# First layer's up groups 4 to 7 in pairs, by seven block products in place of eight

## The chip, the cores and the metric

The kernel runs on one core of a Trainium2 chip. The metric is the device time of one execution in microseconds; before the change it is 982.56 us, the median of 3 runs (982.32 to 982.68). All arithmetic is float32.

## The reference

Two layers of a first block (a mixer with two branches, then an MLP) are followed by a second block. Sequence length is 256, width 1024, inner width 4096. What matters here is the first block's MLP, once for each of two layers; `rms` stands for the normalisation:

```
u = relu(rms(x) * g_mlp @ w_up) ** 2      # [256, 1024] @ [1024, 4096]
x = x + u @ w_down                        # [256, 4096] @ [4096, 1024]
```

The scale of a row is left out of the products and put on the result, since the square makes it a factor of the row.

## The kernel before

**Three products for one.** A float32 product is made of three matmuls on a shorter format. Each operand is split into an upper part (a rounded copy) and a lower part (the remainder): upper times upper, upper times lower, lower times upper. Of weights, a *piece* is 128 partitions x 4 blocks x 512 columns (1 MB). ScalarE copies it into `w_hi` (`split` at L1737), VectorE subtracts that from the loaded piece into `w_lo` (`split` at L2160). Both rings hold three pieces (`SPLIT_RING`), so the split of piece p waits until TensorE has used piece p − 3.

**TensorE.** The 256 rows are two tiles of 128. One piece with one tile of rows is 4 blocks x 3 = 12 matmuls of 128x128 by 128x512, called a *block product* here; the first 8 of a piece need only `w_hi`, the last 4 `w_lo` (`products_upper`, L964 to L983). Each group f of `w_up` (512 columns) has two pieces, so four block products and 48 matmuls (`mlp_up`). `mlp_down` adds the same number into four banks that stay open. `MLP_STEPS` sets the order: up 0, 1, 2, down 0, up 3, down 1, up 4 and so on.

**Rows of a group.** ScalarE takes the relu from PSUM (L1895), VectorE multiplies it by the bank (L2388) into `u_rows`, SyncE stores the rows to `u_bounce` and fetches them back by blocks of 32 (`store_up`, `fetch_up`), VectorE transposes the blocks (L2336, `up_rows_turn`), ScalarE makes the upper part (L1903) and VectorE the remainder (L2404). Then `mlp_down` can use them.

**Order.** Each engine's order is written out by hand, and each works in that order. ScalarE and VectorE call `step(p)` in a loop over `MLP_STEPS`, which splits piece p + 2; `TURNED_IN` says between which splits a group's rows are transposed. SyncE issues all transfers; a load waits until the piece that lay in its place (a ring of four) has been split by VectorE. GpSimd does nothing in this stage but two short powers.

The first layer's MLP begins at about 201 us; its first up group ends at 212.5, and its last matmul starts at 375.5.

Of the kernel before, what the change touches and what calls it, by code (L numbers as in the profile page):

```python
# [6 lines left out]
F32 = mybir.dt.float32  # L7
# [74 lines left out]
UP_PIECE = [PIECE_MLP + 2 * MLP_STEPS.index(("up", f)) for f in range(F_GROUPS)]  # L82
DOWN_PIECE = [PIECE_MLP + 2 * MLP_STEPS.index(("down", f)) for f in range(F_GROUPS)]
# [3 lines left out]
PIECES = PIECE_MLP + 4 * F_GROUPS  # L87
ANGLES_AT = 2
TURNED_IN = {2: 0, 3: 1, 14: F_GROUPS - 1}
TURNED_IN.update({MLP_STEPS.index(("up", f)) + (3 if f < F_GROUPS - 2 else 2): f for f in range(2, F_GROUPS - 1)})  # L90

# [6 lines left out]
E_PIECE = DEPTH * PIECES  # L98
# [22 lines left out]
RAW_SLOTS = [p % RAW_RING for p in range(RAW_SWITCH)] + list(RAW_ODD)  # L121
# [63 lines left out]
def build_program(nc, ins, consts, where, out):  # L185
    ctx = ExitStack()
    with ctx:
# [86 lines left out]

        def raw_at(p):

            slot = RAW_SLOTS[p]
            if slot < RAW_KEPT:
# [74 lines left out]
        u_bounce = [nc.dram_tensor(f"u_bounce{i}", [T * P, COLS], F32, kind="Internal").ap() for i in range(2)]  # L353
# [151 lines left out]
        up_half = sem("up_half")  # L505
        up_hi = sem("up_hi")
# [89 lines left out]
        def last_piece(n):  # L596

            l, u = divmod(n, USES)
            if l < DEPTH:
                if u < W_IN_GROUPS:  # L600
                    return l * PIECES + 2 * u + 1
                if u in USE_YB:
                    return l * PIECES + PIECE_B[USE_YB.index(u)] + 1
                if u in USE_YA:
                    return l * PIECES + PIECE_A[USE_YA.index(u)]
                if u < USE_UP:
                    return l * PIECES + PIECE_O + 2 * (u - USE_O) + 1
                return l * PIECES + UP_PIECE[u - USE_UP] + 1
# [85 lines left out]
        def _(sp):  # L694
# [7 lines left out]
            def load(piece):  # L702
# [18 lines left out]
                elif p == 2:  # L721
                    sp.dma_start(raw_at(2)[:, 0:KP // 2, :], piece[:, 0:KP // 2, :]).then_inc(third_landed, 16)
# [6 lines left out]
                n[0] += 1  # L729

# [68 lines left out]
            def store_up(l, g):  # L799
# [3 lines left out]
                else:  # L803
                    for t in range(T):
                        sp.wait_ge(out_free[t], l * USES + USE_UP + g + 1)
                store_rows(u_bounce[g % 2].rearrange("(t p) n -> p t n", p=P), u_rows, rows_stored)

            def fetch_up(l, g):

                sp.wait_ge(rows_stored, 16 * (STORES * l + 2 * T + g + 2))  # L810
                sp.wait_ge(blocks_turned, MOVES * l + 2 + g + 1)
                fetch_blocks(u_moved, u_bounce[g % 2], row_blocks)

            def row_blocks_piece(w, c, half):

                return w.rearrange("(p k) n -> p k n", p=P)[:, half * KP:half * KP + KP, c * COLS:(c + 1) * COLS]

            for l in range(DEPTH):
# [14 lines left out]
                for i, (kind, f) in enumerate(MLP_STEPS):  # L833
                    if l == DEPTH - 1 and i == 9:
                        for t in range(T):
                            sp.wait_ge(out_free[t], l * USES + USE_UP)
                        sp.dma_start(g_final, ins["g_final"].partition_broadcast(P)).then_inc(g_first_landed, 16)
                        sp.dma_start(g_pre[0], ins["pre_norm_g_2"][0].partition_broadcast(P)).then_inc(g_first_landed, 16)
                        for b, w in enumerate(("o_c_re_2", "o_c_im_2")):
                            sp.dma_start(c_in[:, b, :, :], ins[w][0].rearrange("(s g) p o -> (g p) s o", g=2)).then_inc(s5_landed, 16)  # L840
                        for b, w in enumerate(("o_b_re_2", "o_b_im_2")):
                            sp.dma_start(b_in[:, b, :, :], ins[w][0].rearrange("(j g) i p -> (g i) j p", g=8)).then_inc(s5_landed, 16)
                    for c in range(2):
                        if kind == "down":
                            load(square_piece(ins["w_down"][l, f * COLS:(f + 1) * COLS, :], c, 0))
                        else:
                            load(square_piece(ins["w_up"][l], f, 1 - c if f == 0 else c))
                        if c == 0 and i >= 4 and MLP_STEPS[i - 4][0] == "up":
                            fetch_up(l, MLP_STEPS[i - 4][1])
                    if i == 1:  # L850
                        store_up(l, X_ROWS)
                        fetch_up(l, X_ROWS)
                    if i >= 3 and MLP_STEPS[i - 3][0] == "up":
                        store_up(l, MLP_STEPS[i - 3][1])
                fetch_up(l, F_GROUPS - 1)
# [77 lines left out]
        def _(pe):  # L933
# [146 lines left out]
            def first_group():  # L1080
# [52 lines left out]
                pe.wait_ge(second_hi, 1)  # L1133
# [2038 lines left out]
```

## Time and profile before

| | |
|---|---|
| median of 3 runs | 982.56 us |
| the profiled execution: its own time | 982.39 us |
| its span, from the first to the last instruction | 980.3 us |
| TensorE busy | 972.4 us, 5186 matmuls |
| VectorE busy | 739.5 us, 831 instructions |
| ScalarE busy | 506.1 us, 605 instructions |
| GpSimd busy | 129.2 us, 101 instructions |
| bytes moved by DMA | 224.77 MB |
| granted TensorE clock, mean | 0.999 of full speed |

Busy time counts overlapping instructions once. In the views below a line starts with the start in us and the duration in us, then engine, line of the kernel, operation and operands (output, then inputs, partitions x elements). "x2" is two instructions merged into one line; what stands in brackets is the idle time before it and who ended it. PE is TensorE, DVE VectorE, ACT ScalarE, POOL GpSimd, SP SyncE.

### The profile page before, as it was taken

The page shows a single profiled execution, that of the slowest core. Times are in us where ns is not written, and L with a number is a line of the kernel's source. Part 1 is how long each engine was busy: PE and PEld are TensorE (multiplying, and loading weights), DVE is VectorE, ACT ScalarE, POOL GpSimd, SP SyncE. Part 2 cuts the span into 40 slices and gives each one's busy share as a digit, 9 for nine tenths or more (in the row PEclk, how much of TensorE's full clock was granted, in tenths as well). Part 3 has the DMA queues.
Part 4 walks back from the last instruction along what each step waited for, and adds up shares of the span by engine and source line. Part 5 has one row for each costly group of instructions (what it writes and reads, how often), then busy time and mean ns, then how long its engine had stood idle before and what let it go on. Part 6 is the DMA issues. An engine that isn't in the chain of part 4 may idle for free.

```text
span 980.3 us, 12877 instructions
## 1 busy us (share of the span) xinstructions
PE 972.4 (99%) x5186; PEld 813.9 (83%) x5186; DVE 739.5 (75%) x831; ACT 506.1 (52%) x605; POOL 129.2 (13%) x101
## 2 busy tenths in 40 slices
PE   9999999999999999999999999999999999999997
PEld 7888888888888888888888888888887899799696
DVE  5878886776555756678787776989777788789984
ACT  6656553564444445455563464544387454644251
POOL 0000000000000000000000001000000159269820
PEclk9999999999999999999999999999999999999999
DMA  9997796678977773697796669799774957446351
GB/s 359 307 281 274 237 274 204 233 231 252 283 245 245 227 244 122 193 304 247 238 274 224 209 229 270 240 290 271 246 248 133 297 181 255 139 164 161 104 193 44
DMA packets 142684, 224.77 MB, mean 229 GB/s; under 512 B 11809, under 2 KB 50721, under 8 KB 142369
## 3 DMA queue, kind: packets, MB, share of 16 engines
q1 hardware_dynamic: 142624, 223.95, 72.6%
q8 instruction: 41, 0.67, 0.3%
q14 instruction: 19, 0.15, 0.0%
HBM read 199.32 MB, written 22.28 MB: 226 GB/s over the span
## 4 chain that ended last, share of the span: by engine, by line
PE 98%; DMA 1%; DVE 0%; ACT 0%; issue 0%; POOL 0%; DVEq 0%; SPq 0%; ACTq 0%
PE bank L949 15%; PE bank L952 15%; PE bank L951 15%; PE bank L972 12%; PE bank L976 12%; PE bank L983 12%; PE bank L1352 2%; PE bank L1649 1%; PE bank L1461 1%; PE bank L1424 1%; PE bank L1087 1%; PE bank L1064 1%; PE bank L1177 1%; PE bank L1636 1%; PE bank L981 1%; PE bank L974 1%
## 5 line engine op out<-in xcount | busy, mean ns | idle before, releaser
L2160 DVE TENSOR_TENSOR w_lo<-raw,w_hi 128x2048 fp32r<-128x2048 f32 (+1 forms) x78 | 178.3, 2290 | 77.4 <-ACT w_hi L1737 77.3
L2160 DVE TENSOR_TENSOR w_lo<-arena,w_hi 128x2048 fp32r<-128x2048 f32 (+1 forms) x79 | 181.5, 2303 | 55.0 <-ACT w_hi L1737 54.8
L1737 ACT ACTIVATE w_hi<-raw 128x2048 fp32r<-128x2048 f32 (+1 forms) x83 | 156.9, 1891 | 89.2 <-PE bank L952 77.8
L1737 ACT ACTIVATE w_hi<-arena 128x2048 fp32r<-128x2048 f32 (+1 forms) x79 | 149.3, 1890 | 82.8 <-PE bank L952 81.0
L949 PE MATMUL bank<-w_hi,hT 128*128 128x512 f32 (+1 forms) x352 | 135.7, 385 | 0.0
L952 PE MATMUL bank<-w_hi,hT 128*128 128x512 f32 (+1 forms) x336 | 129.0, 384 | 0.0
L951 PE MATMUL bank<-w_lo,hT 128*128 128x512 f32 (+1 forms) x336 | 129.0, 384 | 0.0
L972 PE MATMUL bank<-w_hi,hT 128*128 128x512 f32 (+1 forms) x320 | 123.1, 386 | 0.0
L976 PE MATMUL bank<-w_hi,hT 128*128 128x512 f32 (+1 forms) x320 | 122.4, 384 | 0.0
L2929 POOL TENSOR_TENSOR rstd<-mean,const 128x1 f32<-128x1 f32 (+1 forms) x16 | 9.1, 576 | 618.6 <-DVE mean L2169 459.4
L983 PE MATMUL bank<-w_lo,hT 128*128 128x512 f32 (+1 forms) x320 | 83.9, 384 | 0.0
L949 PE MATMUL bank<-w_hi,uT_hi 128*128 128x512 f32 x208 | 81.0, 389 | 0.0
L951 PE MATMUL bank<-w_lo,uT_hi 128*128 128x512 f32 x208 | 80.9, 389 | 0.0
L952 PE MATMUL bank<-w_hi,uT_lo 128*128 128x512 f32 x208 | 80.9, 389 | 0.0
L949 PEld LDWEIGHTS bank<-w_hi,hT 128*128 128x128 f32 x352 | 66.2, 188 | 13.0
L952 PEld LDWEIGHTS bank<-w_hi,hT 128*128 128x128 f32 x336 | 63.1, 188 | 12.5
L951 PEld LDWEIGHTS bank<-w_lo,hT 128*128 128x128 f32 x336 | 63.1, 188 | 12.3
L972 PEld LDWEIGHTS bank<-w_hi,hT 128*128 128x128 f32 x320 | 60.1, 188 | 13.3 <-issue 1.7
L976 PEld LDWEIGHTS bank<-w_hi,hT 128*128 128x128 f32 x320 | 60.1, 188 | 11.6
L983 PEld LDWEIGHTS bank<-w_lo,hT 128*128 128x128 f32 x320 | 59.3, 188 | 11.9
L972 PE MATMUL bank<-w_hi,uT_hi 128*128 128x512 f32 x176 | 68.8, 391 | 0.0
L2336 DVE STREAM_TRANSPOSE arena<-arena 128x1024 f32<-128x1024 f32 (+3 forms) x36 | 47.9, 1330 | 27.5 <-DMA arena<-u_bounce 16.6
(348 smaller groups left out, 1762.1 us busy)
## 6 DMA issues: line engine op xcount, KB each, us to landing
arena<-in_w_in SPq DMA_DIRECT2D x21, 1024.0 KB, 6.0
raw<-in_w_in SPq DMA_DIRECT2D x20, 1024.0 KB, 7.4
arena<-in_w_up SPq DMA_DIRECT2D x16, 1024.0 KB, 6.5
raw<-in_w_up SPq DMA_DIRECT2D x16, 1024.0 KB, 7.3
raw<-in_w_down SPq DMA_DIRECT2D x16, 1024.0 KB, 5.2
arena<-in_w_down SPq DMA_DIRECT2D x16, 1024.0 KB, 5.8
u_bounce<-arena SPq DMA_DIRECT2D x18, 512.0 KB, 6.2
arena<-u_bounce SPq DMA_DIRECT2D x72, 128.0 KB, 5.7
```

What stands on the lines that cost most here:

```text
L949: pe.matmul(dst, a_hi, b_hi, start=first, stop=False, skip_group_check=shared)
L951: pe.matmul(dst, a_hi, b_lo, start=False, stop=False, skip_group_check=shared)
L952: mm = pe.matmul(dst, a_lo, b_hi, start=False, stop=last_one, skip_group_check=shared)
L972: pe.matmul(dst, a_hi, b_hi, start=(start and i == 0), stop=False, skip_group_check=shared)
L974: pe.matmul(dst, a_hi, b_lo, start=False, stop=False, skip_group_check=shared)
L976: pe.matmul(dst, a_lo, b_hi, start=False, stop=False, skip_group_check=shared)
L981: mm = pe.matmul(dst, a_lo, b_hi, start=False, stop=last_one, skip_group_check=shared)
L983: mm = pe.matmul(dst, a_hi, b_lo, start=False, stop=last_one, skip_group_check=shared)
L1352: last = pe.matmul(OUT[t], a[:, k0 + kk, at], w[:, s, kk, :], start=(first and kk == 0), stop=(last_one and kk == KP - 1))
L1737: act.activation(w_hi[:, p % SPLIT_RING, :, 0:n], raw_at(p)[:, :, 0:n], copy).then_inc(hi_ready, 1)
L2160: dve.tensor_tensor(w_lo[:, s, :, 0:n], raw_at(p)[:, :, 0:n], w_hi[:, s, :, 0:n].bitcast(F32), ALU.subtract).then_inc(lo_ready, 1)
L2336: return dve.transpose(dst.rearrange("p s (u q) -> p u s q", q=BLOCK), src.rearrange("p u (s f) -> p u s f", s=slots))
```

## The change

In the first layer, up groups 4 and 5, and 6 and 7, are computed in pairs. Rows tiles t = 0, 1, halves of the inner dimension and the two groups make a 2 by 2 product of blocks: eight block products. They become seven (a Strassen-Winograd scheme). With A the rows (half, tile) and B the pieces of weights, the seven are, in the order in which TensorE makes them:

```
F1: A(1,0) x B11            bank 0     B11: half 1 of the pair's first group
F2: S2     x T3             bank 1     S2 = A(1,0) - A(1,1)        T3  = B22 - B12
F3: A(0,0) x B21            bank 0+    B21: half 0 of the first group
F4: S1     x T2             bank 6     S1 = S0 - A(1,0)            T2  = B22 - B12'
F5: S0     x B12'           bank 7     S0 = A(1,1) + A(0,1)        B12' = B12 - B11
R1: S3     x B22            bank 7+    S3 = A(0,0) - S1
R2: A(0,1) x B21'           bank 1+    B21' = B21 - T2
```

GpSimd makes S0 to S3 once (14 instructions with two inputs of 128x512, and 4 with one input that make upper parts) and T3, B12', T2 and B21' for each pair (one instruction of 128x2048 each), every one waiting for the one before. ScalarE copies bank 0 after F1 and takes its relu after F3. VectorE adds the banks and squares: nine instructions of 128x512 a pair, three of which have both inputs in SBUF. Each of the seven has its own piece to split. The order of steps becomes up 0, 1, 2, 3, first 4 (F1 to F5), down 0, rest 4 (R1, R2), down 1, first 6, down 2, rest 6, down 3 to 7. The pairs' raw pieces get six places of their own; those of pair one are loaded between the pieces of up 2 and up 3. The second layer keeps its order.

Apart from this, the bounce buffers become nine, some semaphores of the very first group are merged into others, and counts are rewritten (`BASE`, `STEP_AT`). The core of the diff:

```diff
+PAIRED_STEPS = [("up", 0), ("up", 1), ("up", 2), ("up", 3), ("first", 4), ("down", 0), ("rest", 4), ("down", 1), ("first", 6),
+                ("down", 2), ("rest", 6)] + [("down", f) for f in range(3, F_GROUPS)]
+TURNED_IN = [{2: 0, 3: 1, 7: 2, 9: 3, 11: 4, 12: 5, 13: 6, 14: 7}, INNER_TURNS]
...
+            def pair_first(l, i):
+                n, p = l * USES + USE_UP + PAIRED[i], FIRST_OF[i]
+                for t in range(T):
+                    pe.wait_ge(out_free[t], n if i else n - 1)
+                pair_product(p, 0, *pair_rows(1, 0), True).then_inc(piece_used, 1)
+                pe.wait_ge(pool_sums, 1)
+                pair_product(p + 1, 1, *pair_sums(2), True).then_inc(piece_used, 1)
+                pe.wait_ge(pair_taken, 2 * i + 1)
+                pair_product(p + 2, 0, *pair_rows(0, 0), False).then_inc(piece_used, 1)
+                for t in range(T):
+                    pe.wait_ge(out_free[t], n)
+                pe.wait_ge(pool_sums, 4)
+                pair_product(p + 3, 6, *pair_sums(1), True).then_inc(piece_used, 1)
+                pair_product(p + 4, 7, *pair_sums(0), True).then_inc(piece_used, 1)
...
+                if p in PAIR_SUMS:
+                    act.wait_ge(pool_sums, PAIR_SUMS[p])
...
+            def pair_one(i):
+                dve.wait_ge(rows_stored, 16 * (2 * T + PAIRED[i] + 1))
+                dve.wait_ge(pair_taken, 2 * i + 2)
+                order.mark(dve.tensor_tensor(by_block(u_rows[:, 0, :]), by_column(pair_c), by_column(bank[:, 0, :]), ALU.mult))
...
+            def pair_third(i):
+                dve.wait_ge(piece_used, REST_OF[i] + 2)
+                order.link(dve.tensor_tensor(by_block(pair_c), by_column(bank[:, 1, :]), by_column(pair_w), ALU.add))
+                square_rows(u_rows[:, 1, :], pair_c).then_inc(out_free[1], 2)
...
+                def weights(dst, a, b):
+                    pool.tensor_tensor(pair_raw(dst), pair_raw(a), pair_raw(b), ALU.subtract).then_inc(pool_sums, 1)
...
+                for i in range(len(PAIRED)):
+                    if i:
+                        pool.wait_ge(middle_landed, 16 + 64)
+                        piece_split(pool, FIRST_OF[0] + 3)
+                        weights(PAIR_T3[1], PAIR_B22[1], PAIR_B12[1])
+                    weight_sum(i, 1)
+                    pool.wait_ge(pair_outer, 32 * (i + 1))
+                    weights(PAIR_B12[i], PAIR_B12[i], PAIR_B11[i])
+                    weight_sum(i, 2)
+                    if i:
+                        piece_split(pool, REST_OF[0] + 1)
+                    pool.wait_ge(pool_sums, 5)
+                    weights(PAIR_T2[i], PAIR_B22[i], PAIR_B12[i])
+                    weight_sum(i, 3)
+                    piece_split(pool, FIRST_OF[i] + 2)
+                    weights(PAIR_B21[i], PAIR_B21[i], PAIR_T2[i])
+                    weight_sum(i, 4)
```

In SyncE's new order the second pair's first load waits for `pool_sums`, ahead of the loads for down 2; the stores of a pair's two groups stand together, and `fetch_up` of a group behind them.

## Rows read from the trace of the kernel before

**Rows 1.** The page, part 1 (busy) and part 4 (chain that ended last).

```profile
PE 972.4 (99%) x5186; PEld 813.9 (83%) x5186; DVE 739.5 (75%) x831; ACT 506.1 (52%) x605; POOL 129.2 (13%) x101
...
PE 98%; DMA 1%; DVE 0%; ACT 0%; issue 0%; POOL 0%; DVEq 0%; SPq 0%; ACTq 0%
```

**Rows 2.** Windows: one stretch of the first layer's MLP, its columns first.

```profile
core 0: us, PE busy (x) PEld busy (x) DVE busy (x) ACT busy (x) POOL busy (x), PEclk, DMA share, GB/s
...
212.50:375.30 162.80, 162.80 (x720) 134.78 (x719) 99.03 (x68) 74.95 (x57) 1.10 (x2) 1.00 0.81 250
```

**Rows 3.** Waits from 200 to 376: total us, times, longest us.

```profile
ACT w_hi L1737 <- PE bank L952: 57.8, 21, 3.5
DVE w_lo L2160 <- ACT w_hi L1737: 45.2, 21, 3.1
```

**Rows 4.** Timeline of TensorE: first matmuls of two successive pieces.

```profile
234.29 0.39 PE L972 MATMUL bank<-w_hi,uT_hi 128*128 128x512 f32 x1
...
239.73 0.39 PE L972 MATMUL bank<-w_hi,uT_hi 128*128 128x512 f32 x1
```

**Rows 5.** Timeline of VectorE in the first layer's MLP.

```profile
206.14 1.67 DVE L2581 SCALAR_TENSOR_TENSOR hT<-arena,vec,hT 128x256 fp32r<-128x256 f32 x4 [0.94 <-ACT hT L1949]
207.73 4.49 DVE L2160 TENSOR_TENSOR w_lo<-raw,w_hi 128x2048 fp32r<-128x2048 f32 x2
...
228.81 2.25 DVE L2160 TENSOR_TENSOR w_lo<-raw,w_hi 128x2048 fp32r<-128x2048 f32 x1
230.99 1.21 DVE L2404 TENSOR_TENSOR uT_lo<-arena,uT_hi 128x1024 fp32r<-128x1024 f32 x1
...
234.32 1.48 DVE L2388 TENSOR_TENSOR arena<-arena,bank 128x512 f32<-128x512 f32 x2
```

**Rows 6.** Timeline of ScalarE: one split.

```profile
245.43 1.92 ACT L1737 ACTIVATE w_hi<-raw 128x2048 fp32r<-128x2048 f32 x1 [2.03 <-PE bank L952]
```

**Rows 7.** GpSimd's groups by line and form: busy us, mean ns, idle before.

```profile
L3092 POOL TENSOR_TENSOR w_lo<-raw,w_hi 128x2048 fp32r<-128x2048 f32 x3 | 13.8, 4612 | 7.2 <-ACT w_hi L1737 4.5 <-DVE w_lo L2160 2.6
...
L3017 POOL TENSOR_TENSOR const<-const,conv_w 128x2048 f32<-128x2048 f32 x1 | 3.7, 3700 | 20.8 <-ACT arena L2006 20.8
...
L2974 POOL TENSOR_SCALAR pool_m<-arena 128x240 f32<-128x240 f32 x4 | 3.6, 890 | 0.2
...
L3017 POOL TENSOR_TENSOR const<-const,conv_w 128x512 f32<-128x512 f32 x1 | 1.0, 1045 | 0.0
```

**Rows 8.** Timelines of GpSimd and VectorE where both work, late in the kernel.

```profile
772.96 3.70 POOL L3017 TENSOR_TENSOR const<-const,conv_w 128x2048 f32<-128x2048 f32 x1 [20.77 <-ACT arena L2006]
773.06 3.68 DVE L2656 TENSOR_TENSOR arena<-arena,const 128x64 f32<-128x64 f32 x1
776.66 0.21 DVE L2657 TENSOR_TENSOR arena<-arena,const 128x64 f32<-128x64 f32 x1
...
864.90 4.60 POOL L3092 TENSOR_TENSOR w_lo<-raw,w_hi 128x2048 fp32r<-128x2048 f32 x1 [4.03 <-ACT w_hi L1737]
866.43 1.23 DVE L2805 TENSOR_TENSOR arena<-bank,arena 128x1024 f32<-128x1024 f32 x1 [3.12 <-PE bank L1620]
...
892.18 6.68 DVE L2160 TENSOR_TENSOR w_lo<-raw,w_hi 128x2048 fp32r<-128x2048 f32 x2
892.64 8.50 POOL L3034 TENSOR_TENSOR h_sb<-arena 128x1024 f32<-128x1024 f32 x2 [0.51 <-PE bank L1636]
...
913.63 4.78 POOL L3034 TENSOR_TENSOR h_sb<-arena 128x1024 f32<-128x1024 f32 x2 [0.41 <-DVE arena L2820]
```

**Rows 9.** Timeline of SyncE: the store of group 0 and its fetch.

```profile
214.12 0.37 SPq L733 DMA_DIRECT2D u_bounce<-arena  x1
...
221.10 1.81 SPq L739 DMA_DIRECT2D arena<-u_bounce  x4
```

**Rows 10.** The last matmul, and the window of the span's end.

```profile
973.82 0.39 PE L952 MATMUL bank<-w_hi,uT_lo 128*128 128x512 f32 x1
...
975.00:980.30 5.30, 0.00 (x0) 0.00 (x0) 2.30 (x5) 0.00 (x0) 0.54 (x1) 0.78 0.50 187
```

More of the change, by code:

```diff
@@ L96 @@
 USES = USE_UP + F_GROUPS
-E_PIECE = DEPTH * PIECES
+E_PIECE = BASE[DEPTH]
 E_OUT_PIECE = E_PIECE + 12
@@ L120 @@
 RAW_ODD = (0, 1, 4, 0, 1, 4, 0, 1, 0, 2, 3, 1, 0)
-RAW_SLOTS = [p % RAW_RING for p in range(RAW_SWITCH)] + list(RAW_ODD)
+RAW_SLOTS = []
+for p in range(RAW_SWITCH):
+    RAW_SLOTS.append(PAIR_PIECES[p] if p in PAIR_PIECES else (p - sum(i < p for i in PAIR_PIECES)) % RAW_RING)
+RAW_SLOTS += RAW_ODD
 RAW_KEPT = 2
@@ new lines, in paired_loads, with up, down @@
+            def paired_loads(l):
+                def up(f, half):
+                    load(square_piece(ins["w_up"][l], f, half))
+                def down(f, c):
+                    load(square_piece(ins["w_down"][l, f * COLS:(f + 1) * COLS, :], c, 0))
+                up(0, 1)
+                up(0, 0)
+                up(1, 0)
+                up(1, 1)
+                store_up(l, X_ROWS)
+                fetch_up(l, X_ROWS)
+                up(2, 0)
+                load_pair(0, PAIR_B12, 1, 1)
+                up(2, 1)
+                load_pair(0, PAIR_B22, 1, 0)
+                up(3, 0)
+                load_pair(0, PAIR_B11, 0, 1)
+                up(3, 1)
+                load_pair(0, PAIR_B21, 0, 0)
+                store_up(l, 0)
+                down(0, 0)
+                fetch_up(l, 0)
+                down(0, 1)
+                store_up(l, 1)
+                down(1, 0)
+                fetch_up(l, 1)
+                down(1, 1)
+                store_up(l, 2)
+                fetch_up(l, 2)
+                store_up(l, 3)
+                sp.wait_ge(pool_sums, SUM_COUNTS[0][1])
+                piece_split(sp, FIRST_OF[0])
+                load_pair(1, PAIR_B12, 1, 1)
+                piece_split(sp, FIRST_OF[0] + 1)
+                load_pair(1, PAIR_B22, 1, 0)
+                sp.wait_ge(pool_sums, SUM_COUNTS[0][2])
+                piece_split(sp, FIRST_OF[0] + 4)
+                load_pair(1, PAIR_B11, 0, 1)
+                down(2, 0)
+                down(2, 1)
+                piece_split(sp, REST_OF[0])
+                load_pair(1, PAIR_B21, 0, 0)
+                down(3, 0)
+                down(3, 1)
+                fetch_up(l, 3)
+                store_up(l, 4)
+                store_up(l, 5)
+                down(4, 0)
+                down(4, 1)
+                fetch_up(l, 4)
+                down(5, 0)
+                down(5, 1)
+                store_up(l, 6)
+                store_up(l, 7)
+                fetch_up(l, 5)
+                down(6, 0)
+                down(6, 1)
+                fetch_up(l, 6)
+                down(7, 0)
+                down(7, 1)
+                fetch_up(l, 7)
@@ L832, in _ @@
                     load(square_piece(ins["w_out"][l], c, 1))
[L833 to L855, printed above, removed]
+                (paired_loads if l == 0 else mlp_loads)(l)
             def store_qk2(i):
@@ L1536, in _ @@
                 mlp_first(l)
-                for kind, f in MLP_STEPS[1:]:
+                for kind, f in STEPS[l][1:]:
                     if kind == "up":
                         mlp_up(l, f)
+                    elif kind == "first":
+                        pair_first(l, PAIRED.index(f))
+                    elif kind == "rest":
+                        pair_rest(l, PAIRED.index(f))
                     elif l == DEPTH - 1 and f == F_GROUPS - 1:
```

312 lines of the change are left out of this document (237 added, 75 removed).

## The prediction, before the kernel was run

> **What bounds the kernel now.** I read the page's busy times and chain first: TensorE is busy 972.4 of 980.3 us and makes 98% of the chain that ends last [rows 1]. So time leaves the kernel only with matmuls, and comes back whenever TensorE must wait. Then the windows of the stage that changes: from 212.5 to 375.3 TensorE is busy all of 162.8 us, VectorE 99.0, ScalarE 75.0, GpSimd 1.1 [rows 2]. The waits of that stage say who follows whom: ScalarE's splits wait for TensorE (57.8 us), VectorE's for ScalarE (45.2 us), and TensorE, busy throughout, for neither [rows 3]. Last, the timelines, for what the change puts on VectorE and on GpSimd, and the places late in the kernel where both read SBUF at once.
>
> **What it removes.** 24 matmuls start 5.44 us apart in two successive half pieces of that stage [rows 4], 0.2267 us each. A block product is 12 matmuls, 2.72 us; eight become seven twice, so 24 matmuls go: −5.4 us. Nothing in it is doubtful, as TensorE had no wait there.
>
> **What it adds on VectorE and ScalarE, taken alone.** Each pair needs seven splits of a piece (F1 to F5, R1, R2) where two groups needed four: six more of 2.2 us on VectorE (4.49 us for two, [rows 5]) and of 1.9 on ScalarE [rows 6]. The results cost nine instructions of some 0.7 us a pair on VectorE in place of four squares of that length. Together about 13 + 7 = 20 us on an engine with 64 us idle in that stage; ScalarE has 88 us idle. In a "first" block TensorE takes 13.6 us; VectorE's five splits and two results take 12.5 and ScalarE's five splits and two copies 10.8. That fits, and a remainder is wanted only 8 matmuls (1.8 us) after its upper part. Alone I price this at 0 to 1 us, never below nothing, since TensorE had no wait there to lose. The first group's merged semaphores keep their order and the bounce buffers, now nine, lie in HBM: both nothing, beside the same work as before.
>
> **What it adds on GpSimd.** Rows: 14 two-input instructions of 128x512 and 4 one-input copies of 128x512. Weights: 8 subtractions of 128x2048. None of these is in the trace. A subtraction with two contiguous inputs of 128x2048 takes 4.6 us, one with broadcast views 3.7; 128x512 takes 1.05; a one-input one of 240 elements 0.89 [rows 7]. I take 4.6 (the nearest row; end 3.7), 1.2 with its gap (a quarter of 4.6 is 1.15; end 1.05) and 1.6 (between 0.89 as it is and 1.9 scaled up). That is 16.8 + 6.4 + 36.8 = 60 us, with the low ends 14.7 + 3.6 + 29.6 = 48.
>
> The GPSIMD Engine Reference of the Trainium skill (§4.1) says that one-input instructions go at roughly line rate. By that the four copies would take some 0.5 us each, an estimate by that page, and the sum below would be about 4 us less; the trace's 0.89 us for 240 elements disagrees.
>
> **Who excludes whom.** Late in the kernel both engines read SBUF at once. A VectorE instruction of 64 columns, 0.21 us just after, takes 3.68 us from just behind the start of a 3.70 us GpSimd one. Two splits take 6.68 us in place of 4.49, and two GpSimd instructions beside them 8.50, where two such take 4.78 undisturbed: they take turns, one whole instruction each [rows 8]. A VectorE instruction with one operand in PSUM (1.23 us) runs through a GpSimd subtraction that keeps its 4.60 us [rows 8]. So splits and remainders of rows (both inputs in SBUF) take turns with all of GpSimd's new work; results with a PSUM operand don't, nor, I take it, transposes.
>
> The Trainium skill (SBUF — State Buffer, § Who interferes with whom) states this rule: a VectorE instruction with two SBUF inputs and a GpSimd one that reads SBUF hold a shared port for a whole instruction. It speaks against the change; the trace agrees. Without the rule the answer is the first rival's.
>
> **The sum, by taking turns.** GpSimd can begin when the turned columns are split, at 205.2.
> (a) Up to F4's remainder. F4's weights are made of all before them: 16.8 + 6.4 + three weight subtractions 13.8 = 37.0 us of GpSimd. VectorE needs, before the split of F4, the rows' remainder 1.6, nine splits (pieces 2 to 10 of the stage) 19.9 and two remainders of rows 2.3: 23.8 [rows 5]. One after another they end at 205.2 + 60.8 = 266.0, and F4's own split at 268.2. TensorE wants it at 245.2 (end of the four up groups) + 8.2 (F1 to F3) + 1.8 = 255.2. Late by 13.0.
> (b) F5 and the piece after it: VectorE's split waits one weight subtraction each time (R2's, then the second pair's first): 4.6 + 2.2 = 6.8 us a piece where TensorE takes 2.7: 2 x 4.1 = 8.2.
> (c) The two pieces of down group 1 beside the second pair's next two subtractions: 6.8 against 5.44: 2.7. The last subtraction falls into a gap.
> (d) The second pair's first product waits until bank 1 is read. Behind the last late split VectorE has two results 1.4, a transpose 1.2, a split 2.2, a remainder 1.1, two results 1.4 = 7.3; TensorE has 16 matmuls, 3.6: late by 3.7. ScalarE's copy of the second pair's bank 0 then waits for the store of pair one, with the splits of F3 and later queued behind it: 1.6 (0 to 5).
> (e) The fetch of group 5 is queued behind two stores; VectorE's transpose of it has the splits behind it: 1.4.
> Together 13.0 + 8.2 + 2.7 + 3.7 + 1.6 + 1.4 = 30.6, less 5.4: **+25.2 us**. The profiled execution of before took 982.39 us (span 980.3), 0.17 under the median of 982.56, so 982.4 + 25.2 = **1007.6 us**.
>
> **Transfers and waits.** Bytes are unchanged, but four loads of 1 MB move ahead, between 200 and 213. The store of group 0 now stands behind twice the loads: issued at 214.12, it had landed by 221.10 [rows 9]; by some 6 us later its transpose, with piece 6's split behind it, uses up the 5 us by which that split (ended 231.1, [rows 5]) beat TensorE (236.1). That costs about 1 us at its place, but the lateness at F4 already contains it. GpSimd's sums make SyncE wait before the second pair's loads; behind stand down group 2's, wanted 40 us later. TensorE's own new waits, for the row sums (ready about 251) and for ScalarE's copy, come before the weights that are later still.
>
> **The rivals.**
> 1. *They don't exclude each other in this stage* (another memory region, short instructions slip in). Then GpSimd's 60 us run free and are ready some 8 us early; what is left is −5.4, the transfers' 1 to 2, the tight first block's 1 and (e) 1.4: −1.7, **980.7 us**. For it: VectorE's idle share. Against: rows 8, with no exception among them. 8%. That all 5.4 us are saved (977.0): 2%.
> 2. *GpSimd is at its low ends.* (a) 14.7 + 3.6 + 11.1 = 29.4 for 37.0, so 5.4 late; (b) and (c) 0.9 less for each of 3.7-us turns: 6.4 and 0.9; (d), (e) 6.7: 19.4 − 5.4 = +14: **996.4 us**. For it: the 3.70 us row; against: three rows of 4.6 us on contiguous operands. 18%.
> 3. *TensorE's clock falls in the new gaps.* After the last matmul at 974.2 the granted clock averages 0.78 over the last 5.3 us [rows 10], so within such an idle stretch it falls from 2.4 to 1.2 GHz. My gaps reach 4 to 6 us. If it falls three times and a block product (2.7 us at the upper level) doubles each time: +8, **1015.7 us**. Against: part of the slower matmuls hides in what is late anyway. 17%.
> The TensorE page of the Trainium skill (Part 1, the HAM clock gate) says the same of idle stretches; it adds nothing to the sum.
> 4. *Half-way*: turns are taken, but GpSimd's row sums fit into idle VectorE time so well that only (b) to (d) bite: 16 − 5.4, **993 us**. 10%.
>
> **How the numbers follow.** Forecast case (1003 to 1011) 43%, cheap GpSimd or half-way (990 to 1003) 28%, clock or more queueing (1011 to 1020) 17%, below 982 10%, the rest 2%. The range 990 to 1018 leaves out the no-exclusion case and the far end. About 0.2% (2 us) is what a measurement of this kernel can tell from no change. Of the 10% below 982, 980.7 lies at that bound: faster by more 6%, within it 4%, slower 90%.
>
> **What would show it.** Right: TensorE gaps of some us between 236 and 315, none before; VectorE's splits there at 3.4 to 6.8 us instead of 2.3, while GpSimd is busy; GpSimd's 128x2048 subtractions at 4.6 to 6.9; F4's remainder ending near 268; the end of the layer near 401 instead of 375.8; later stages shifted as a whole. Wrong: splits still at 2.3 us beside a busy GpSimd (rival 1), 24 matmuls fewer and no gaps; or gaps that end on a DMA instead of VectorE; or GpSimd well under 48 us.

## The result and the profile after

The changed kernel takes **1005.52 us** (median of 4 runs, 1004.83 to 1006.22) against 982.46 (982.32 to 982.68, 4 runs) on the same chip: ratio 1.0234, 95% interval [1.0217, 1.0252]. It is 23.1 us slower; the forecast was 1007.6, in a range of 990 to 1018. The profiled execution took 1006.22 us (span 1004.3). One execution behind the times below stands apart and is in none of the ratios: of the five of run 1 one took 1973.68 us, the other four 978.0 to 979.9.

The page after, parts 1 and 4, for [rows 1]:

```profile
PE 978.4 (97%) x5162; PEld 815.5 (81%) x5162; DVE 793.5 (79%) x847; ACT 514.6 (51%) x607; POOL 212.9 (21%) x127
...
PE 89%; DVE 5%; DMA 3%; issue 1%; ACT 1%; SPq 0%; POOL 0%; DVEq 0%; ACTq 0%
```

The 24 matmuls are gone, and yet TensorE is *busier* by 6 us, and the chain that ended last leaves it for VectorE. VectorE gained 54.0 us of busy time for 17.8 us of new work (what it gains in run 1, below), GpSimd 83.7 for 61. The waits of TensorE from 200 to 402 (total us, times, longest):

```profile
PE bank L1100 <- DVE w_lo L2343: 12.9, 6, 4.2
PE bank L1089 <- issue: 3.4, 1, 3.4
PE bank L1512 <- DVE hT L2811: 2.4, 1, 2.4
```

Before there were none in this stage. They sum to 18.7 us. The first layer's last addition stands at 400.38 in place of 375.93 (24.4 later); what follows is shifted nearly as a whole (the span ends 24.0 later). 24.4 + 5.4 saved − 18.7 leaves 11.1 us, which the windows of the stage explain (columns as in [rows 2]):

```profile
245.00:250.00 5.00, 4.61 (x21) 3.49 (x19) 4.08 (x2) 2.79 (x2) 4.92 (x3) 1.00 0.88 293
250.00:260.00 10.00, 4.60 (x12) 3.32 (x12) 10.00 (x3) 0.78 (x3) 8.09 (x2) 0.83 0.23 52
260.00:270.00 10.00, 8.49 (x31) 6.94 (x32) 10.00 (x6) 9.07 (x8) 5.00 (x1) 0.83 0.64 203
270.00:280.00 10.00, 5.91 (x18) 4.00 (x16) 10.00 (x3) 3.42 (x2) 7.24 (x2) 0.83 0.48 165
280.00:290.00 10.00, 9.67 (x35) 7.80 (x36) 9.32 (x8) 1.92 (x1) 0.00 (x0) 0.83 0.85 298
...
310.00:320.00 10.00, 7.20 (x19) 5.76 (x20) 6.99 (x6) 4.39 (x4) 2.76 (x1) 0.66 0.55 155
```

The reader is to see three things. VectorE is busy all of 250 to 280, where TensorE has 61 matmuls instead of the 132 that 30 us hold at 0.2267 us each. Second, the granted clock: 0.83 for a window of 10 us means 3.4 us of it at the lower of the two levels (1.2 in place of 2.4 GHz), 0.66 means 6.8: some 20 us in all. Three of the five falls come just behind a wait of TensorE (4.2, 2.4 and 2.0 us), two near the end of one (3.1 and 3.4 us). A matmul there takes twice as long, so about 10 us of TensorE's time went that way. Third, GpSimd is at work beside most of it. Side by side, VectorE and then GpSimd, between 205 and 280 (and GpSimd's last subtraction, which nothing disturbs):

```profile
205.94 4.32 DVE L2811 SCALAR_TENSOR_TENSOR hT<-arena,vec,hT 128x256 fp32r<-128x256 f32 x4 [0.94 <-ACT hT L2120]
...
215.68 1.27 DVE L2571 TENSOR_TENSOR arena<-arena,bank 128x512 f32<-128x512 f32 x2
216.88 3.45 DVE L2352 SCALAR_TENSOR_TENSOR mean<-ssq 128x1 f32<-128x1 f32 x2
...
245.92 1.25 DVE L2519 STREAM_TRANSPOSE arena<-arena 128x1024 f32<-128x1024 f32 x1 [1.77 <-DMA arena<-u_bounce]
247.09 6.65 DVE L2343 TENSOR_TENSOR w_lo<-arena,w_hi 128x2048 fp32r<-128x2048 f32 x1
253.67 5.58 DVE L2587 TENSOR_TENSOR uT_lo<-arena,uT_hi 128x1024 fp32r<-128x1024 f32 x1
259.18 2.28 DVE L2343 TENSOR_TENSOR w_lo<-arena,w_hi 128x2048 fp32r<-128x2048 f32 x1
261.38 1.27 DVE L2571 TENSOR_TENSOR arena<-arena,bank 128x512 f32<-128x512 f32 x2
262.57 11.12 DVE L2343 TENSOR_TENSOR w_lo<-arena,w_hi 128x2048 fp32r<-128x2048 f32 x3
273.62 0.68 DVE L2605 TENSOR_TENSOR arena<-h_sb,bank 128x512 f32<-128x512 f32 x1
274.21 6.06 DVE L2343 TENSOR_TENSOR w_lo<-arena,w_hi 128x2048 fp32r<-128x2048 f32 x1
```

```profile
213.57 6.67 POOL L3318 TENSOR_TENSOR arena<-arena 128x2048 f32<-128x2048 f32 x1
220.19 1.30 POOL L3313 TENSOR_TENSOR arena<-hT 128x512 f32<-128x512 f32 x1
221.45 3.33 POOL L3314 TENSOR_TENSOR arena<-hT 128x512 f32<-128x512 f32 x1
...
247.02 11.15 POOL L3318 TENSOR_TENSOR arena<-arena 128x2048 f32<-128x2048 f32 x2
265.00 6.54 POOL L3318 TENSOR_TENSOR arena<-arena 128x2048 f32<-128x2048 f32 x1 [6.83 <-DVE w_lo L2343]
272.43 5.70 POOL L3318 TENSOR_TENSOR arena<-arena 128x2048 f32<-128x2048 f32 x1 [0.89 <-DMA arena<-in_w_up]
...
317.24 4.62 POOL L3318 TENSOR_TENSOR arena<-arena 128x2048 f32<-128x2048 f32 x1 [13.96 <-DVE w_lo L2343]
```

The split at 247.09 takes 6.65 us: GpSimd's subtraction began 0.07 us earlier, and the split itself is the 2.28 us of the one at 259.18, where GpSimd was idle. The remainder behind it (1.21 in [rows 5]) takes 5.58 for the same reason. TensorE's timeline shows what that makes it wait for: the lower matmuls of F1, F2, F5 and of down 0's first piece.

```profile
253.80 1.81 PE L1100 MATMUL bank<-w_lo,hT 128*128 128x512 f32 x4 [4.19 <-DVE w_lo L2343]
261.51 2.08 PE L1100 MATMUL bank<-w_lo,sum_hi 128*128 128x512 f32 x4 [3.11 <-DVE w_lo L2343]
...
268.43 1.07 PE L1100 MATMUL bank<-w_lo,sum_hi 128*128 128x512 f32 x4
...
273.75 1.37 PE L1100 MATMUL bank<-w_lo,sum_hi 128*128 128x512 f32 x4 [2.44 <-DVE w_lo L2343]
...
280.33 1.21 PE L1100 MATMUL bank<-w_lo,uT_hi 128*128 128x512 f32 x4 [1.98 <-DVE w_lo L2343]
...
312.80 0.77 PE L1089 MATMUL bank<-w_hi,hT 128*128 128x512 f32 x1 [3.38 <-issue]
```

### The profile page after: what moved, and what is told of

Its sections match the earlier page's. It is cut to its first block, busy times and chain, and to the rows that moved or that the text cites. A ratio compares the mean times of both kernels' runs of the same rounds, so it can differ in the third digit from the quotient of the medians.

```text
span 1004.3 us, 12900 instructions
## 1 busy us (share of the span) xinstructions
PE 978.4 (97%) x5162; PEld 815.5 (81%) x5162; DVE 793.5 (79%) x847; ACT 514.6 (51%) x607; POOL 212.9 (21%) x127
## 4 chain that ended last, share of the span: by engine, by line
PE 89%; DVE 5%; DMA 3%; issue 1%; ACT 1%; SPq 0%; POOL 0%; DVEq 0%; ACTq 0%
PE bank L1066 14%; PE bank L1068 13%; PE bank L1069 13%; PE bank L1089 12%; PE bank L1100 11%; PE bank L1093 11%; DVE w_lo L2343 3%; PE bank L1813 1%; PE bank L1512 1%; DMA arena<-u_bounce 1%; PE bank L1621 1%; PE bank L1584 1%; DMA u_bounce<-arena 1%; PE bank L1204 1%; PE bank L1181 1%
## 5 line engine op out<-in xcount | busy, mean ns | idle before, releaser
L2343 DVE TENSOR_TENSOR w_lo<-arena,w_hi 128x2048 fp32r<-128x2048 f32 (+1 forms) x89 | 219.2, 2474 | 45.8 <-ACT w_hi L1908 45.5
L1908 ACT ACTIVATE w_hi<-arena 128x2048 fp32r<-128x2048 f32 (+1 forms) x89 | 168.3, 1893 | 91.0 <-PE bank L1069 81.5
L1908 ACT ACTIVATE w_hi<-raw 128x2048 fp32r<-128x2048 f32 (+1 forms) x79 | 149.2, 1890 | 68.4 <-PE bank L1069 54.6
L1089 PE MATMUL bank<-w_hi,hT 128*128 128x512 f32 (+1 forms) x312 | 121.4, 391 | 3.4 <-issue 3.4
L1066 PE MATMUL bank<-w_hi,hT 128*128 128x512 f32 (+1 forms) x320 | 123.2, 385 | 0.0
L1093 PE MATMUL bank<-w_hi,hT 128*128 128x512 f32 (+1 forms) x312 | 120.5, 388 | 0.0
L1069 PE MATMUL bank<-w_hi,hT 128*128 128x512 f32 (+1 forms) x304 | 116.6, 384 | 0.0
L1068 PE MATMUL bank<-w_lo,hT 128*128 128x512 f32 (+1 forms) x304 | 116.6, 383 | 0.0
L3172 POOL TENSOR_TENSOR rstd<-mean,const 128x1 f32<-128x1 f32 (+1 forms) x16 | 12.7, 800 | 419.2 <-DVE mean L2352 260.0
L1100 PE MATMUL bank<-w_lo,hT 128*128 128x512 f32 (+1 forms) x312 | 83.3, 390 | 4.2 <-DVE w_lo L2343 4.2
L1069 PE MATMUL bank<-w_hi,uT_lo 128*128 128x512 f32 x208 | 81.5, 392 | 0.0
L1089 PEld LDWEIGHTS bank<-w_hi,hT 128*128 128x128 f32 x312 | 59.5, 191 | 17.0 <-issue 5.4
L1100 PEld LDWEIGHTS bank<-w_lo,hT 128*128 128x128 f32 x312 | 58.6, 191 | 16.4 <-DVE w_lo L2343 4.6
L1066 PEld LDWEIGHTS bank<-w_hi,hT 128*128 128x128 f32 x320 | 60.2, 188 | 11.7
L1093 PE MATMUL bank<-w_hi,uT_lo 128*128 128x512 f32 x176 | 69.3, 394 | 0.0
L1093 PEld LDWEIGHTS bank<-w_hi,hT 128*128 128x128 f32 x312 | 59.5, 191 | 11.6
L1069 PEld LDWEIGHTS bank<-w_hi,hT 128*128 128x128 f32 x304 | 57.1, 188 | 11.2
```

The costliest lines, as they stand in the source:

```text
L1066: pe.matmul(dst, a_hi, b_hi, start=first, stop=False, skip_group_check=shared)
L1068: pe.matmul(dst, a_hi, b_lo, start=False, stop=False, skip_group_check=shared)
L1069: mm = pe.matmul(dst, a_lo, b_hi, start=False, stop=last_one, skip_group_check=shared)
L1089: pe.matmul(dst, a_hi, b_hi, start=(start and i == 0), stop=False, skip_group_check=shared)
L1093: pe.matmul(dst, a_lo, b_hi, start=False, stop=False, skip_group_check=shared)
L1100: mm = pe.matmul(dst, a_hi, b_lo, start=False, stop=last_one, skip_group_check=shared)
```

## The experiments

The theory: VectorE's instructions with two inputs in SBUF and GpSimd's that read SBUF take turns, one whole instruction each, and VectorE, late by that, makes TensorE wait. Rivals: the other parts of the change cost the time; TensorE waits for GpSimd's results, not for the turns; the lower clock costs it. The kernel before took 982.4 to 982.6 us (median) beside each of the three sets of runs; every ratio below is against it.

**1. All of GpSimd's sums on 16 columns.** Left out: the sums beyond 16 columns (the products take unsummed rows, and blocks that are summed in 16 columns a row block only). Order, splits, results and waits stay.

```diff
-pool.tensor_tensor(pair_raw(dst), pair_raw(a), pair_raw(b), ALU.subtract)
+pool.tensor_tensor(pair_raw(dst)[:, :, 0:4], pair_raw(a)[:, :, 0:4], pair_raw(b)[:, :, 0:4], ALU.subtract)
```
(and so with the row sums)

Expected: 

> The changed kernel, in which every sum of GpSimd covers 16 columns instead of 512 or 2048, and the products take plain rows in place of the row sums; counts and waits as they are. Theory (GpSimd and VectorE take turns at SBUF, and that alone makes TensorE late): only the 24 matmuls fewer, the store that waits behind twice the loads and the tight first block remain: 981 us (979.5 to 983), VectorE's splits at 2.3 us, no wait of TensorE over 2 us. Rival (VectorE's 20 us more work, the moved loads, or the new waits make it late): 990 us or more, with gaps in the blocks of both pairs.

Measured: 978.5 us, ratio 0.9962 [0.9946, 0.9978]; TensorE's waits in the stage 0.3 us. That is below the 979.5 to 983 I expected. So everything but GpSimd's work is cheap: 3.9 of the 5.4 us are saved. The missing 1.5 us lies in the first pair's block: its lower parts of F1 to F3 begin 0.2 to 0.5 us late each, and F4 starts at 254.84, where 36 matmuls from 245.06 on would reach it at 253.2; VectorE is busy all of 245 to 259 there. 978.5 is also about what the change could give at best in this order.

**2. and 3. Only the row sums, or only the weight sums, on 16 columns.** The same edit, in one of the two places.

Expected of the row sums small: 

> Only the row sums cut to 16 columns (plain rows in the products); the eight weight subtractions whole. Theory of turns: GpSimd's 23 us of row sums go from the time before the fourth product, but each split that meets a weight subtraction still takes up to 6.8 us: 996 us (992 to 1000), two gaps near 4 us at the fifth product and the first piece of down group 0. Rival (it is the length of the chain of sums before the fourth product that costs, not the turns): 984 us or less, as the chain is then 23 us shorter than TensorE needs.

Measured: 995.7 us, ratio 1.0133 [1.0113, 1.0153].

Expected of the weight sums small: 

> Only the eight weight subtractions cut to 16 columns; row sums whole. Theory of turns: VectorE waits 1.2 to 1.6 us a turn, which pieces of 5.4 us can bear: 986 us (984 to 990), the wait behind the split of the first rows (2.4 us) stays. Rival (the number of GpSimd's instructions costs, whatever their length): 995 us or more, since 18 of 26 stay whole.

Measured: 981.6 us, ratio 0.9991 [0.9980, 1.0001]; the wait at 210 (2.4 us) is there, little else.

Above the 978.5 of run 1, the weight sums alone cost 17.2 us, the row sums alone 3.1, both together 27.0. Together they cost more than their sum; that the rows use up the slack that the weights then lack is my reading, which no run tests. The row sums are cheaper than I expected (984 to 990). I take it that 18 short turns fit into VectorE's idle time where 8 long ones don't.

**4. The weight sums as memsets.** Each subtraction becomes three writes of zeros to the same place; left out: the weight sums.

```diff
-pool.tensor_tensor(pair_raw(dst), pair_raw(a), pair_raw(b), ALU.subtract).then_inc(pool_sums, 1)
+for i in range(3):
+    last = pool.memset(pair_raw(dst), 0.0)
+    ...
+last.then_inc(pool_sums, 1)
```

Expected: 

> Each weight subtraction is replaced by three memsets of the same 128x2048 place, one after the other, so GpSimd is about as busy but reads nothing from SBUF; the weights are zeros then. Theory (turns are taken only where GpSimd reads SBUF and VectorE has both inputs there): splits beside memsets take 2.3 us and the time is near that with the subtractions cut away, 986 us (984 to 991), a little later where the chain of sums is late by itself. Rival (any GpSimd instruction stops VectorE's): splits beside memsets longer than 3 us, 995 us or more.

Measured: 983.4 us, ratio 1.0002 [0.9992, 1.0012], at the low edge of what I expected. VectorE, and then GpSimd, in that run:

```profile
248.50 2.25 DVE L2343 TENSOR_TENSOR w_lo<-arena,w_hi 128x2048 fp32r<-128x2048 f32 x1
250.67 1.22 DVE L2587 TENSOR_TENSOR uT_lo<-arena,uT_hi 128x1024 fp32r<-128x1024 f32 x1
251.80 2.28 DVE L2343 TENSOR_TENSOR w_lo<-arena,w_hi 128x2048 fp32r<-128x2048 f32 x1
...
260.47 4.49 DVE L2343 TENSOR_TENSOR w_lo<-arena,w_hi 128x2048 fp32r<-128x2048 f32 x2 [2.99 <-ACT w_hi L1908]
```

```profile
247.32 16.79 POOL L3319 MEMSET arena<- 128x2048 f32 x9
```

This is the run that separates turns from results most sharply. GpSimd is busy *longer* for a sum (5.6 us, a third of the 16.79 below, in place of 4.6), the consumers wait for it just the same, and yet the splits keep their 2.28 us and 22 us are gone: 1.8 us are left over run 3, where the sums are short. What differs is that these instructions of GpSimd read nothing. The same run bounds another rival, the loads that SyncE holds back for GpSimd's sums: they wait here as before. The SBUF page of the Trainium skill (SBUF — State Buffer, § Who interferes with whom) ties the exclusion to a GpSimd instruction that reads SBUF; the memsets, which only write there, bear it out.

**5. The kernel before, with the same GpSimd work that nobody needs.** 14, 4 and 8 instructions, the subtractions on constant tables, no one waiting. They begin at 207.9, as in run 10, and the last seven subtractions follow one another from 258.1 to 301.3, where the changed kernel spreads them up to 321.9.

```diff
+for i in range(n):
+    order.link(pool.tensor_tensor(block[2], block[0], block[1], ALU.subtract))
```
(and the short ones on 128x512)

Expected: 

> The kernel before, unchanged in its matmuls, splits and transfers; GpSimd additionally does the change's instructions (14 two-input and 4 one-input ones of 128x512, 8 subtractions of 128x2048) on constant tables from the same moment on, and nobody waits for any of them. Turn-taking theory: the cost comes back though no result of GpSimd is used, since VectorE's splits and remainders are held up all the same: eight subtractions take eight turns of 4.6 us, the 18 short ones take some 23 us of turns, and VectorE has some 60 us idle in the stage but not where it matters: 1003 us (997 to 1008), with splits of up to 6.9 us and TensorE waits on w_lo. Dependency theory (TensorE waits for GpSimd's results, or for ScalarE's splits of the sums): 982.5, no waits.

Measured: 992.8 us, ratio 1.0104 [1.0084, 1.0124]. Turns alone make the *unchanged* kernel 10.2 us slower, with splits of up to 6.7 us: the mechanism is there. But it is below the 997 to 1008 I expected, half of the cost. The same instructions cost 10 us here and 25 in run 9. Two things differ, and no run parts them: here VectorE has 64 us idle in the stage and each piece gives it 5.44 us, against 2.72 in a first block; and the dates of the subtractions are not the same. VectorE, and then GpSimd, in this run:

```profile
220.17 2.29 DVE L2160 TENSOR_TENSOR w_lo<-arena,w_hi 128x2048 fp32r<-128x2048 f32 x1 [1.92 <-ACT w_hi L1737]
...
257.69 1.25 DVE L2336 STREAM_TRANSPOSE arena<-arena 128x1024 f32<-128x1024 f32 x1
258.86 6.02 DVE L2160 TENSOR_TENSOR w_lo<-arena,w_hi 128x2048 fp32r<-128x2048 f32 x1
264.81 5.63 DVE L2404 TENSOR_TENSOR uT_lo<-arena,uT_hi 128x1024 fp32r<-128x1024 f32 x1
270.36 6.68 DVE L2160 TENSOR_TENSOR w_lo<-arena,w_hi 128x2048 fp32r<-128x2048 f32 x1
```

```profile
219.50 1.50 POOL L3075 TENSOR_SCALAR arena<-arena 128x512 f32<-128x512 f32 x1
...
258.11 29.97 POOL L3079 TENSOR_TENSOR arena<-const 128x2048 f32<-128x2048 f32 x5
```

The first lines of the two show an exception to the theory: the split at 220.17 begins 0.8 us before the end of one of GpSimd's one-input copies and keeps its 2.29 us. The same is seen in the changed kernel, where the split at 210.18 begins 0.7 us before the end of the copy at 209.31 and takes 2.28; in run 3 a split that begins 0.24 us behind the start of a copy takes 2.51. So a copy that is under way holds a split up little or not at all; the two-input sums do the harm.

**6. Weight sums in quarters.**

```diff
-pool.tensor_tensor(pair_raw(dst), pair_raw(a), pair_raw(b), ALU.subtract)
+for k in range(KP):
+    last = pool.tensor_tensor(pair_raw(dst)[:, k, :], pair_raw(a)[:, k, :], pair_raw(b)[:, k, :], ALU.subtract)
```

Expected: 

> The changed kernel with each weight subtraction of 128x2048 as four of 128x512. Turns of one whole instruction: a split of 2.3 us then waits for at most one quarter (1.2 us) in place of 4.6, while GpSimd's own end comes later because each of its quarters may wait for a VectorE instruction; the first pair is freed most: 998 us (994 to 1002), splits beside GpSimd at 2.3 to 3.5 us, a quarter at 1.2 to 3.5. Rival, in which GpSimd's late results are what costs: 1008 or more, since its sums end later.

Measured: 996.2 us, ratio 1.0138 [1.0118, 1.0159]. Same elements, 9.3 us less: a turn is one instruction, so a quarter holds up a split by about 1.1 us (3.18 and 3.38 us for the splits of F1 and F2, of which the first took 6.65). GpSimd pays: 2.36 us a quarter, 74.5 us for 8 sums in place of 46, and TensorE now has a wait of 5.6 us that ends on ScalarE's split of a sum that comes late (F4's weights). Here results do cost something.

**7. TensorE kept at work in the gaps.** 32 upper matmuls are done again (7.3 us), where it waited.

```diff
+for again in range({FIRST_OF[0]: 2, FIRST_OF[0] + 1: 1, FIRST_OF[0] + 4: 1}.get(p, 0)):
+    ...
+        pe.matmul(dst, u_hi, v_hi, start=(i == 0), stop=False, skip_group_check=True)
+        pe.matmul(dst, u_lo, v_hi, start=False, stop=False, skip_group_check=True)
```

Expected: 

> The changed kernel in which TensorE repeats, before it waits for the remainder, the 8 upper matmuls of three products (two more times for the first product of pair one, once more for its second and its fifth; each restarted, so the result is the same). The repeats lie in stretches where TensorE waited anyway. Clock theory (some 24 us of the stage ran at 1.2 GHz after the waits, about 10 us of slower matmuls): the waits are as before or shorter by what is filled, the fall is put off, and the time is 5 to 8 us less: 999 us (996 to 1002). Rival (the slower matmuls hide in what VectorE is late with): 1005.5, with the granted clock at 1.00 and the waits longer by the same amount.

Measured: 1005.2 us (1004.4 to 1007.6), ratio 1.0234 [1.0219, 1.0249]: no difference from the changed kernel. TensorE's waits in the stage come to 13.7 us for 18.7. The clock stayed at 1.00 up to 260 (0.83 from 250 on in the changed kernel), and fell only later:

```profile
250.00:260.00 10.00, 7.79 (x35) 6.12 (x33) 10.00 (x2) 3.93 (x6) 9.34 (x2) 1.00 0.20 52
260.00:270.00 10.00, 8.38 (x25) 6.74 (x26) 10.00 (x6) 4.96 (x4) 4.89 (x1) 0.66 0.64 204
```

But F2's lower matmuls start at the same date, and so do down 0's:

```profile
261.62 2.08 PE L1100 MATMUL bank<-w_lo,sum_hi 128*128 128x512 f32 x4 [3.83 <-DVE w_lo L2348]
...
280.55 1.57 PE L1100 MATMUL bank<-w_lo,uT_hi 128*128 128x512 f32 x4 [3.21 <-DVE w_lo L2348]
```

261.62 and 280.55 against 261.51 and 280.33: those dates are VectorE's. 7.3 us of extra matmuls fitted in for nothing, so that much of TensorE's time between 245 and 280 was free, whether it waited or went slowly. My theory that the clock adds 5 to 8 us falls for that stretch. It did not keep the clock up throughout, so what the slower matmuls between 281 and 290 and at 312 cost is left open.

**8. All sums on VectorE.** The same instructions in VectorE's stream, ahead of the splits.

```diff
 def step(p):
+    for job in JOBS.get(p + AHEAD, ()):
+        job()
     split(p + AHEAD)
```
(each job: a row sum with its parts, or a weight sum, with `dve` in place of `pool`)

Expected: 

> The changed kernel with all row and weight sums on VectorE in place of GpSimd, in the order of its stream, each ahead of a split. Turn-taking theory: 8 subtractions at 2.3 and 18 short instructions at about 0.6 cost VectorE some 29 us, less than the 60 us for which GpSimd's excluded it. With sums on 16 columns VectorE had 15.8 us idle from 213 to 245, nothing from 245 to 270, some 7.8 from 270 to 300, and it gets about 17, 2.3 and 9.2 more: 978.5 plus 1.2, 2.3, 1.4: 983 us (980 to 987). Rival (what counts is only how long the sums take after the up groups, or VectorE's load): over 990.

Measured: 989.8 us (989.0 to 992.8), ratio 1.0083 [1.0064, 1.0101]. A miss by 7 us. A sum costs VectorE 2.29 us and a row instruction 0.69, as I took it; what I left out was their place. TensorE's waits in it:

```profile
228.67 1.21 PE L1100 MATMUL bank<-w_lo,hT 128*128 128x512 f32 x4 [2.52 <-DVE w_lo L2343]
...
244.86 1.95 PE L1100 MATMUL bank<-w_lo,hT 128*128 128x512 f32 x4 [4.97 <-DVE w_lo L2343]
```

The sums ahead of a split make the raw places come free later; SyncE's loads wait for those (the one issued at 212.07 in run 1 goes out at 219.15, behind a split that ends at 219.1), and the fetch of the rows is queued behind the loads. VectorE then stood 4.66 us before its transpose, with a weight sum and a split behind it.

**9. The changed kernel, with sums that nobody reads.** GpSimd does the same amount and writes all but the first weight sum to one spare place; ScalarE and TensorE wait for the loads only. Left out: the sums in the products.

```diff
-return sum_hi[:, i, :, :], sum_lo[:, i, :, :]
+return pair_rows(*((1, 1), (1, 0), (1, 0), (0, 0))[i])
...
-act.wait_ge(pool_sums, PAIR_SUMS[p])
+act.wait_ge(middle_landed, 48 + 32 * second)
+act.wait_ge(pair_outer, 32 * (1 + second))
```

Expected: 

> The changed kernel in which no engine reads a sum: GpSimd does the same 14, 4 and 8 instructions, but the products take the unsummed rows and blocks, and ScalarE and TensorE wait only for the loads (GpSimd itself, and SyncE's loads into the blocks that it reads, wait as before). Left out: the sums in the products. If the cost is in the turns alone, the same instructions hold up VectorE's splits as before and the time stays near the changed kernel's: 1001 us (997 to 1006). If it is in the waiting for GpSimd's results (F4's weights, ready near 260), it falls towards the run with sums of 16 columns: 978.5 and 2.5 for the early wait, 981 to 986. In between, the share of each can be read: the cost found here is the turns', the rest of 1005.5 the results'.

Measured: 1003.6 us (2 runs, 1003.2 to 1003.9), ratio 1.0213 [1.0192, 1.0233]. Of the 27.0 us that GpSimd's work costs, 25 come without anyone on ScalarE or TensorE waiting for its results; the other 2 would be that waiting, and as this interval overlaps the changed kernel's [1.0217, 1.0252], they are not clear of the noise. F2's lower matmuls begin at nearly the same date (261.51 in the changed kernel), behind one wait in place of two:

```profile
260.94 2.08 PE L1102 MATMUL bank<-w_lo,hT 128*128 128x512 f32 x4 [8.58 <-DVE w_lo L2344]
```

**10. The row sums begin later.**

```diff
 pool.wait_ge(turned_lo, 4 * (PHASES * l + MLP_PHASE) + 4)
+pool.wait_ge(up_lo, l * ROWS_MOVED + 1)
```

Expected: 

> The changed kernel, with GpSimd's first row sums only after VectorE has written the remainder of the turned rows (one wait more). It takes away the first wait on TensorE's path, at 210.3, where four short VectorE instructions took 4.3 us in place of 1.7. Theory: GpSimd's chain starts some 2.5 us later and the date of F4's split (268) is set by the sum of GpSimd's and VectorE's work, so what is saved at 210 is given back at F4: 1005 us (1003 to 1007), no wait at 210 and longer ones at 250 to 275. Rival: the early wait is a cost of its own, 1003.0.

Measured: 1004.1 us (2 runs, 1003.7 to 1004.6), ratio 1.0219 [1.0198, 1.0239]. The wait of 2.4 us at 210 is gone. The time is 1.4 us less, halfway between the two expectations; the interval overlaps the changed kernel's, so the run doesn't decide between them. The waits have moved: the longest, 9.8 us, now ends on ScalarE's split for F4.

```profile
PE bank L1089 <- ACT w_hi L1908: 9.8, 1, 9.8
PE bank L1100 <- DVE w_lo L2343: 6.3, 6, 1.8
PE bank L1089 <- issue: 3.3, 1, 3.3
```

F4 begins at 266.28 here and at 266.61 in the changed kernel. So the time returns under another name. VectorE is held up less before F4 here, but GpSimd more: it finishes F4's weights at 264.2, for 258.2 in the changed kernel, and VectorE itself stands 10.9 us before F4's split. In this run it is a result of GpSimd that TensorE waits for, late by the turns that went to VectorE.

**11. All sums on VectorE, each behind the splits.** As run 8, with other places; the splits of the stage's seventh and ninth pieces go ahead of the transpose.

```diff
+ahead = l == 0 and i in (2, 3)
+if ahead:
+    step(q)
 if i in TURNED_IN[l]:
     up_rows_turn(l, TURNED_IN[l][i])
```

Expected: 

> All sums on VectorE as in the run before, but placed behind the splits instead of ahead of them (rows of the outer sum and the first weight sum behind the splits and squares of groups 0 and 1, the rounded copies behind the square, the two next weight sums around the second transpose), and the splits of pieces 6 and 8 of the stage go ahead of the transpose that waits for its fetch. In the run before the first wait (2.5 us) stood behind row sums and the second (5.0 us) behind a transpose that waited 4.7 us for rows whose loads the late splits had held up; 1.7 us more went with the clock that fell there. Theory: those 9 us become about 3, since VectorE has some 17 us idle from 205 to 245 for 17.8 us of sums: 983 us (980 to 986), the same as before the change. Rival (VectorE is simply full): 988 or more.

Measured: 985.6 us (10 runs, 984.0 to 986.4), ratio 1.0026 [1.0016, 1.0035]. No wait before 245, and three of 4.5 us together from 249 to 258:

```profile
249.63 0.47 PE L1089 MATMUL bank<-w_hi,sum_hi 128*128 128x512 f32 x1 [1.71 <-ACT w_hi L1908]
252.15 1.19 PE L1100 MATMUL bank<-w_lo,sum_hi 128*128 128x512 f32 x4 [0.46 <-DVE w_lo L2343]
257.75 1.97 PE L1100 MATMUL bank<-w_lo,hT 128*128 128x512 f32 x4 [2.29 <-DVE w_lo L2343]
```

This takes back 20 of the 23 us and still loses 3.1 to the kernel before. VectorE does all sums in about 29 us where they take GpSimd 61; but from 213 to 257.7 it is idle for only 2.4 us, and the bound of run 1 leaves only 3.9 us to win. No version here that makes all the sums beats the kernel before.

## Why the prediction was right

The mechanism that the forecast rests on, turns of whole instructions at SBUF, is what the runs show, and it sets nearly all of the cost. That 1007.6 came within 2.1 us of 1005.5 is in part luck: the path to it was another one, a wait was missed, the clock was left out of the sum, and smaller terms made up for it.

**The terms of GpSimd's work** held. A weight subtraction that is left alone takes 4.62 us (4.6 taken), a short row instruction 1.28 to 1.33 (1.2), a copy 1.49 to 1.55 (1.6): 61 us for 60. The low ends of rival 2 are out. Rival 1, no exclusion, is out by runs 4 and 5. A copy from f32 to fp32r of 128x512 at 1.49 us is three times the 0.5 that I had estimated from the Trainium skill (GPSIMD Engine Reference, §4.1): there the measurement decides.

**(a) and (b)** gave TensorE's lateness. In run 1 the first pair begins at 245.06; at 0.2267 us a matmul F4's lower matmuls would follow at 255.0 and those of down 0 at 260.5. They start at 268.43 and 280.33: late by 13.4 us, predicted 13.0, and by 19.9, predicted 21.2. The way there was another. I had VectorE and GpSimd one after another up to F4's split, which ends at 268.2 and makes TensorE wait 13 us there. In the trace that split ends at 267.05, before TensorE wants it, and F4 has no wait of its own: TensorE has lost 2.4 us at 210, 4.2 at F1 and 3.1 at F2, the rest is slower matmuls. The reason I gave, that F4's weights are made of all before them, was not the working one in this kernel: run 9 drops that dependence and saves some 2 us. It is in runs 6 and 10, where TensorE waits 5.6 and 9.8 us for ScalarE's split of those weights. That the sum held all the same fits the turns, which make each engine give the other its time: from 205.08 to 258.17 GpSimd is at work without a pause, 53.1 us for some 38 us of its own work.

**Missed: the first wait.** I counted the turned rows' remainder as 1.6 us inside (a). It is four instructions of 0.48 us, which took 0.72, 1.51, 1.49 and 0.83 us beside GpSimd's row sums: 4.3 us together, and TensorE stands 2.4 at 210.31, where I had said that no gap comes before 236. Run 10 takes the wait away and is 1.4 us faster, within the noise; the rest is contained in F4's date.

**(c)** 2.7 predicted, 0.3 + 0.9 measured. **(d)** 3.7 predicted, 3.4 measured, at its place (312.80). It goes with VectorE's lateness: runs 1, 3, 4, 8 and 11 don't have it. **The copy's 1.6 and (e) 1.4** don't appear as waits. Whether the queueing is absent or covered by other lateness, no run shows.

**Rival 3, the clock,** happened in full: about 20 us at the lower level. I had it on top of the waits, for 8 us, and gave it 17%. It lies largely *inside* them: predicted waits 30.6, measured 18.7 of waits and 11.1 of slower work and small stumbles, 29.8 together. Run 7 shows why they exchange from 245 to 280: while VectorE sets the dates, TensorE may wait or creep.

**−5.4** is the one term that is smaller in effect: run 1 brings 3.9 of it, the tight first block takes 1.5, where I priced it at 0 to 1 and left it out of the sum.

## What to carry to other kernels

Before work goes to an idle GpSimd, ask what VectorE reads at that time: where VectorE has both inputs in SBUF and GpSimd runs two-input instructions on SBUF, their times add up, whatever their idle shares say. It cost most where VectorE was already dense (25 us in run 9 against 10 in run 5, where the dates differ too). Two probes decide it, each in one run: the same GpSimd work on constants in the old kernel, and the same time spent in memsets in the new one. And where a late engine sets the dates, don't add a fallen clock to the waits: ask first whether slower work fits into them.

## What the runs showed of the hardware

- A turn is one instruction, whatever its size. Of a pair of 128x1 instructions on VectorE (0.22 us in run 1) the first waited out a 128x2048 subtraction on GpSimd, 3.39 us, and the second took 0.15. Four short ones beside four of GpSimd's took 4.32 us for 1.67.
- GpSimd's one-input copies of 128x512 (1.49 to 1.55 us) are an exception: splits that began 0.7 and 0.8 us before the end of one kept their 2.28 and 2.29 us (210.18 in the changed kernel, 220.17 in run 5). VectorE makes the same copy in 0.43 us in run 8.
- A GpSimd memset of 128x2048 takes 1.81 us (1.87 with its gap) and holds up no split (2.28 us beside nine of them). A transpose with one input kept its time beside a GpSimd row sum (1.25 at 245.92), and so did additions with a PSUM operand beside a subtraction (1.27 for two at 215.68).
- Exclusion works both ways: GpSimd's 4.62 us became 6.67 behind a split that was under way, and 11.15 for two with one split between.
- TensorE's granted clock fell to the lower level behind the waits of 4.2, 2.4 and 2.0 us that end at 253.80, 273.75 and 280.33, and near the end of those of 3.1 and 3.4 us, while the kernel before gave such a fall only at the idle end of [rows 10]. Behind the wait of 2.4 us at 210 it stayed at 1.00; behind the same wait in run 4 (2.3 us) it fell (0.51 from 213.0 to 216.5). The length of the wait alone doesn't tell.
